# A residual block with two mixers: sums of squares over partitions taken from two rounded parts

## The reference

```python
mod = silu(c) @ w_ada + b_ada; shift, scale, gate = split(mod, 3)
h = rms_norm(x, g_pre) * (1 + scale) + shift
hq, hf, hi, hg, dq, dk, dv, dg, ma, mb = split(h @ w_in)
# branch A, 4 heads: gated linear recurrence, 128 x 128 state
o_a = rms_norm(hgrn2_chunked(hq, k(hf), hi, log_f(hf)), hg_norm_gain) * silu(hg)
# branch B, 4 heads: softmax(q1 k1) v - lam * softmax(q2 k2) v, causal
o_b = rms_norm(diff_attention(dq, dk, dv, lam), diff_norm_gain) * (1 - lam_init) * silu(dg)
y = (sigmoid(ma) * (o_a @ w_branch_a) + sigmoid(mb) * (o_b @ w_branch_b)) @ w_out
return x + gate * rms_norm(y, g_post)
```

## Time and profile before

| | us |
|---|---|
| median of 3 runs | 891.16 (889.34 to 892.09) |
| the profiled execution, its own time | 888.69 |
| its span | 886.8 |
| TensorE busy | 843.5 (95%) |
| VectorE busy | 608.5 (69%) |
| GpSimd busy | 478.4 (54%) |
| ScalarE busy | 471.7 (53%) |

### The profile page before, as it was taken

The page is one execution under the profiler, slowest core; times in us unless marked ns, Lnnn a source line. Parts: engine busy times, 40 slices in busy tenths (PEclk is TensorE's granted clock), DMA queues, the critical chain, the costliest instruction groups (busy, mean ns, idle before and its releaser), DMA issues. The chain is left out here.

```text
span 886.8 us, 13086 instructions
## 1 busy us (share of the span) xinstructions
PE 843.5 (95%) x4781; PEld 664.3 (75%) x4781; DVE 608.5 (69%) x712; ACT 471.7 (53%) x861; POOL 478.4 (54%) x363
## 2 busy tenths in 40 slices
PE   2899889999999999999999999999999999999997
PEld 2687678777777777777777777777788888887885
DVE  3888984788794888694897866864500166697775
ACT  7676323786443875445865336745455641333453
POOL 6054685455464455554545653566787822236884
PEclk9899899999999999999999999999999999999999
DMA  9914131102101101110120121021211561302222
GB/s 327 342 45 147 50 94 48 49 1 72 49 15 58 48 14 59 49 48 24 48 72 1 49 72 32 17 72 49 71 48 48 180 224 47 95 24 95 96 95 95
DMA packets 75586, 68.11 MB, mean 77 GB/s; under 512 B 3652, under 2 KB 65156, under 8 KB 75524
## 3 DMA queue, kind: packets, MB, share of 16 engines
q1 hardware_dynamic: 75408, 67.25, 23.6%
q10 hardware_dynamic: 116, 0.03, 0.0%
HBM read 58.88 MB, written 8.39 MB: 76 GB/s over the span
## 5 line engine op out<-in xcount | busy, mean ns | idle before, releaser
L624 POOL TENSOR_TENSOR w_lo<-w_raw,w_hi 128x512 fp32r<-128x512 f32 x140 | 193.5, 1384 | 258.7 <-ACT w_hi L1197 257.2
L935 PE MATMUL pj<-b_hi,w_hi 128*128 128x512 f32 x712 | 299.7, 421 | 6.3 <-DVE dk L1599 3.4
L937 PE MATMUL pj<-b_hi,w_lo 128*128 128x512 f32 x712 | 279.6, 393 | 0.0
L936 PE MATMUL pj<-b_lo,w_hi 128*128 128x512 f32 x712 | 279.0, 392 | 0.0
L935 PEld LDWEIGHTS pj<-b_hi,w_hi 128*128 128x128 f32 x712 | 134.4, 189 | 49.3 <-issue 12.5
L937 PEld LDWEIGHTS pj<-b_hi,w_lo 128*128 128x128 f32 x712 | 134.2, 188 | 30.0
L936 PEld LDWEIGHTS pj<-b_lo,w_hi 128*128 128x128 f32 x712 | 134.8, 189 | 25.6 <-issue 3.1
L1197 ACT ACTIVATE w_hi<-w_raw 128x512 fp32r<-128x512 f32 x132 | 82.8, 627 | 63.5 <-PE pj L937 57.4
L605 POOL TENSOR_TENSOR w_raw<-w_raw,w_raw 128x512 f32<-128x512 f32 x66 | 91.2, 1382 | 2.9
L685 POOL TENSOR_TENSOR wb_lo<-wb_raw,wb_hi 128x512 fp32r<-128x512 f32 x16 | 22.7, 1422 | 63.3 <-ACT wb_hi L1267 63.3
L1212 ACT ACTIVATE p<-sp,cols 128x1024 f32<-128x1024 f32 (+7 forms) x64 | 46.9, 738 | 0.8
(11 more groups left out here) (290 smaller groups left out, 1647.3 us busy)
## 6 DMA issues: line engine op xcount, KB each, us to landing
w_raw<-in_w_in SPq DMA_DIRECT2D x96, 256.0 KB, 4.1
x_in<-in_x SPq DMA_DIRECT2D x8, 512.0 KB, 7.2
ada<-in_w_ada SPq DMA_DIRECT2D x16, 256.0 KB, 7.1
ada<-in_w_ada SPq DMA_DIRECT2D x8, 512.0 KB, 8.0
ada_g<-in_w_ada SPq DMA_DIRECT2D x8, 512.0 KB, 3.9
res<-in_x SPq DMA_DIRECT2D x8, 512.0 KB, 4.4
out_x<-rows_o SPq DMA_DIRECT2D x7, 512.0 KB, 2.9
o_kepta<-oa SPq DMA_DIRECT2D x4, 512.0 KB, 6.0
```

What stands on the lines that cost most here:

```text
L624: pool.tensor_tensor(w_lo[slot(v)][:, :], raw[:, :], w_hi[slot(v)][:, :].bitcast(F32), ALU.subtract).then_inc(s_wlo, 1)
L935: pe.matmul(bank[:, :], wh, part(bh, kk), start=(fresh and kk == 0), stop=False, skip_group_check=True)
L936: pe.matmul(bank[:, :], wh, part(bl, kk), start=False, stop=False, skip_group_check=True)
L937: last = pe.matmul(bank[:, :], wl, part(bh, kk), start=False, stop=(kk == 3), skip_group_check=True)
```

## The change

The sums over partitions (two `ssa` and two `ssb` for each of four heads, 16 in all) were one float32 matmul of 128x512 with `ones`. Now ACT rounds the squares to fp32r (`sqa_hi`, `sqb_hi`), DVE subtracts that from the squares (`sqa_lo`, `sqb_lo`, written over the squares), and PE adds both parts with two fp32r matmuls with `ones_r`. `ones_r` is a rounded copy of `ones`, made once by ACT near the start. The sums move: `ssa` from 61, 63 to 62, 64 and `ssb` from 34, 50 to 35, 52; the first `over` of the recurrence from 63 to 65, the second half of the attention's norm from `over` 51, root 53, `finish` 54 to 53, 55, 56. The buffers of the new parts lie in space that other steps use, and waits are added for that.

```diff
-SSB_AT = (34, 50)
-CLIPB_AT, SQB_AT, OVERB_AT, ROOTB_AT, FINB_AT = (30, 45), (31, 46), (42, 51), (45, 53), (46, 54)
+SSB_AT = (35, 52)
+SQH_A_AT, SQL_A_AT, SQL_B_AT = (60, 61), (61, 62), (33, 49)
+CLIPB_AT, SQB_AT, OVERB_AT, ROOTB_AT, FINB_AT = (30, 45), (31, 46), (42, 53), (45, 55), (46, 56)
-VT_AT, KT_AT, ST_AT, O_AT, SSA_AT = (21, 26), (50, 51), (53, 54), (56, 57), (61, 63)
-CLIPA_AT, SQA_AT, OVERA_AT, ROOTA_AT, FINA_AT = (58, 59), (59, 60), (63, 70), (73, 73), (75, 76)
+VT_AT, KT_AT, ST_AT, O_AT, SSA_AT = (21, 26), (50, 51), (53, 54), (56, 57), (62, 64)
+CLIPA_AT, SQA_AT, OVERA_AT, ROOTA_AT, FINA_AT = (58, 59), (59, 60), (65, 70), (73, 73), (75, 76)
...
                 elif name == "ssa":
-                    pe.wait_ge(s_sqa, 2 * h + n + 1)
-                    last = pe.matmul(by[:, :], ones[:, :], k[:, n * HALF:(n + 1) * HALF], start=True, stop=True)
+                    pe.wait_ge(s_sqal, 2 * h + n + 1)
+                    pe.matmul(by[:, :], ones_r[:, :], part(sqa_hi, n), start=True, stop=False)
+                    last = pe.matmul(by[:, :], ones_r[:, :], part(sqa_lo, n), start=False, stop=True)
                 elif name == "ssb":
-                    pe.wait_ge(s_sqb, 2 * h + n + 1)
-                    last = pe.matmul(bx[:, :], ones[:, :], (sig, p1)[n][:, 0:HALF], start=True, stop=True)
+                    pe.wait_ge(s_sqbl, 2 * h + n + 1)
+                    pe.matmul(bx[:, :], ones_r[:, :], sqb_hi[h][n][:, :], start=True, stop=False)
+                    last = pe.matmul(bx[:, :], ones_r[:, :], sqb_lo[n][:, :], start=False, stop=True)
...
+            act.wait_ge(s_const, N_CONST)
+            act.activation(ones_r[:, :], ones[:, :], ACT.Copy).then_inc(s_sigc, 1)
...
+                    if h:
+                        act.wait_ge(s_unit["ssa"], 2 * h)
                     act.activation(part(v_tok, n), bx[:, :], ACT.Copy).then_inc(s_xa, 1)
...
+                for h, e in recurrence(m, SQH_A_AT):
+                    act.wait_ge(s_unit["o"], 2 * h + 2)
+                    act.wait_ge(s_sqa, 2 * h + e + 1)
+                    act.activation(part(sqa_hi, e), part(k, e), ACT.Copy).then_inc(s_sqah, 1)
...
                     act.activation(t, t, ACT.Square, scale=DOWN).then_inc(s_sqb, 1)
+                    if e == 0 and h < HEADS - 1:
+                        act.wait_ge(s_oah, 2 * h + 2)
+                    if h == HEADS - 1:
+                        act.wait_ge(s_unit["pv" if e else "o"], (NT if e else 2) * HEADS)
+                    elif e:
+                        act.wait_ge(s_unit["ssb"], 2 * h + 1)
+                    act.wait_ge(s_sqb, 2 * h + e + 1)
+                    act.activation(sqb_hi[h][e][:, :], t, ACT.Copy).then_inc(s_sqbh, 1)
...
+                        if h:
+                            dve.wait_ge(s_unit["ssb"], 2 * h)
...
+                for h, e in recurrence(m, SQL_A_AT):
+                    dve.wait_ge(s_sqah, 2 * h + e + 1)
+                    dve.tensor_tensor(part(sqa_lo, e), part(k, e), part(sqa_hi, e).bitcast(F32), ALU.subtract).then_inc(s_sqal, 1)
+                for h, e in attention(m, SQL_B_AT):
+                    dve.wait_ge(s_sqbh, 2 * h + e + 1)
+                    dve.tensor_tensor(sqb_lo[e][:, :], (sig, p1)[e][:, 0:HALF], sqb_hi[h][e][:, :].bitcast(F32),
+                                      ALU.subtract).then_inc(s_sqbl, 1)
```

More of the change, by code:

```diff
@@ L240, in build @@
         v_tok = block_at("v_tok", 40)
+        sqa_hi = block_at("sqa_hi", 40, 1, F32R)
+        sqa_lo = block_at("sqa_lo", 37, 1, F32R)
         f2 = block_at("f2", 41, 0.5)
@@ L255, in build @@
         sig = block_at("sig", 54, 0.5)
+        sqb_hi = [[block_at("sqb_hi", 41.5, 0.5, F32R)] * 2] * (HEADS - 1)
+        sqb_hi.append([block_at(f"sqb_hi_last{e}", (39, 50)[e], 0.5, F32R) for e in range(2)])
+        sqb_lo = [block_at("sqb_lo0", 54, 0.5, F32R), block_at("sqb_lo1", 49, 0.5, F32R)]
         vec_rows = block_at("vec_rows", 52, 1, F32, [P, P])
@@ L295, in build @@
         ones = small("ones", P)
+        ones_r = small("ones_r", P, F32R)
         cols = small("cols", 256)
@@ L383, in build @@
         s_sqa = sem("s_sqa")
+        s_sqah, s_sqal = sem("s_sqah"), sem("s_sqal")
+        s_sqbh, s_sqbl = sem("s_sqbh"), sem("s_sqbl")
         s_rva, s_rvb = sem("s_rva"), sem("s_rvb")
@@ L452, in y_free @@
                 eng.wait_ge(s_unit["dvt"], 2 * HEADS)
-            elif e == 5:
+            elif e == 6:
+                eng.wait_ge(s_unit["ssb"], 2 * HEADS - 1)
+            elif e in (2, 5):
                 eng.wait_ge(s_unit["ssa"], 2 * HEADS)
@@ L1549, in _ @@
             dve.wait_ge(s_gain, 1)
-            dve.wait_ge(s_sigc, 3)
+            dve.wait_ge(s_sigc, 4)
             dve.wait_ge(s_const, N_CONST)
```

## The result

The changed kernel takes **918.27 us** (median of 4 runs, 916.48 to 920.48), the kernel before in the same runs 891.62 us (4 runs, 889.34 to 892.23): the ratio is 1.0317, with a 95% interval of 1.0291 to 1.0342 (the two medians alone give 1.0299). The execution that was profiled took 920.48 us, with a span of 918.6 us.

A forecast was written before the change was run, and what follows sets the result against it. It took TensorE's instruction stream as the bound, busy 843.5 of 886.8 us. The terms -3.8 + 15.8 + 9.0 + 12.4 + 0.2 = +33.6 us gave 922.3 or 924.8, said as 923 us; range 907 to 934.

The forecast's parts named there:

- The matmuls, -3.8: PE's 16 sums: 0.40 us saved each, 6.4 in all, less 2.6 given back by three in slot 50; net -3.8 us.
- The first sum of the recurrence, +15.8: Slot 62, four heads: PE waits 3.95 us each for parts whose rounding stands behind the exponentials on ACT; +15.8 us.
- Slots 52 to 57, +9.0: Heads two to four: PE waits 1.8 us for states at first outputs, 1.2 for `oa` at second; +9.0 us.
- The clock, +12.4: Behind slot 62's four waits: each brings a fall of the granted clock to 0.50, costing 3.1 us; +12.4 us.
- `ones_r`, +0.2: Near the start: one 128x128 copy on ACT, 0.1 to 0.3 us, taken as +0.2.
- DVE's subtraction for slot 35, "0 to 0.3, three times, taken as 0": DVE's subtraction in slot 33 ends just about when PE comes to slot 35; 0 to 0.3 us, taken as 0.
- the sum by it, 3.5 us lower: The sum if the Trainium skill's under 1% held: clock penalty at most 8.9 us in all, the sum 3.5 us lower.
- the signs listed: Idle time of some 3.7 us at slot 62, waits in slots 56 and 57, new matmuls 0.23 us apart, low clock.
- The low clock for some 6 us behind each: Sign: granted clock 0.50 for some 6 us behind each of the four waits in slot 62.
- "Four more digits below 9": Sign: four more digits below 9 in the profile's row of PE's clock over 40 slices.
- The rival without falls of the clock: Waits come in slots 62, 56 and 57, clock stays: +21.2 us, 910 to 912; chance 0.12 with fewer or no falls.

The follow-up runs named there:

- filled kernel: The changed kernel with 14 more matmuls on PE ahead of the recurrence's first sum in each head, output the same: 910.13 us, ratio 1.0234 to the kernel before.
- second execution: The changed kernel run once more, with nothing altered: 917.92 us, ratio 1.0317 to the kernel before.
- better version: Against the kernel before, only `ssa` in slot 64 and `ssb` in slot 35 split, 8 of 16 sums: 886.54 us (ratio 0.9961), again 886.04 (0.9976).

## Why the prediction was right, and where not

The forecast was 923.0 with a range of 907 to 934, slower; 918.3 came. Mechanism, places and sign were right; one term was too large.

- **The matmuls, -3.8:** the ledger gives -3.7 (13 x -0.88, 13 x 0.45, 3 x 0.62). A float32 sum at 0.86 and two rounded at 0.46 are borne out by the kernel with doubled sums. That the three of slot 50 give nothing is in the ledger.
- **The first sum of the recurrence, +15.8:** 15.5 in four waits of 4.04, 3.82, 3.84 and 3.81. That it is the rounding's place behind the exponentials is shown by the kernel that puts it ahead of them.
- **Slots 52 to 57, +9.0:** 4.8 + 3.7 = 8.5 by the ledger, with waits of 1.6 (taken: 1.8) and 1.2 (taken: 1.2). The kernel with the moves alone shows them without any rounding.
- **The clock, +12.4:** the term that was mis-sized. Behind the four new waits four falls came, as taken; the waits of 1.6 and 1.2 brought none. But the four cost 8.5 us and not 12.4. The term took each at the 6.6 us of the earlier trace rows, all of it behind the wait. Two lasted 3.4 us, and of the 6.8 us of the long ones 1.4 and 1.1 us lay in the idle time, where a slow clock costs nothing. Half of what lies behind the wait, 5.5 and 5.7 us and twice 3.3 to 3.4, is 2.7 to 2.9 and 1.7; the filled kernel shows 2.6, 2.7 and 1.6. So the price was right (3.1 of 6.6 us is 0.47, and so are the measured ones), and the length behind the wait was mis-sized. For the short ones the prediction had no row, though the trace of before has one, at 50 to 53 us (granted clock 0.50).
- **`ones_r`, +0.2:** nothing in the ledger stands against it; it is too small to be seen in a start that varies by 1 us.
- Not in the sum: some 0.2 us in each slot 62, which the filled kernel has too. Its slots 62 and 63 cost 3.61; add the 0.87 saved in slot 63, take off 0.45 for the pair and 3.82 for the wait.
- **DVE's subtraction for slot 35, "0 to 0.3, three times, taken as 0":** it came as 0.17, which makes the pair 0.62 in place of 0.45 (counted with the matmuls above). In heads 1 to 3 DVE ends `sqb_lo` 0.15 us ahead of the pair, and the pair starts 0.32 us behind the matmul ahead of it, not 0.23. In the last head `sqb_lo` is done 2.5 us ahead, and the pair takes 0.45. The list of waits shows no idle time as short as this. From the timeline of the changed kernel, first head:

```profile
238.77 0.69 DVE L1780 TENSOR_TENSOR sqb_lo<-sig,sqb_hi 128x512 fp32r<-128x512 f32 x1
239.29 0.39 PE L950 MATMUL pj<-b_hi,w_lo 128*128 128x512 f32 x1
239.61 0.47 PE L831 MATMUL bx<-sqb_hi,ones_r 128*128 128x512 f32 x1
```

So -3.7 + 15.5 + 8.5 + 8.5 + 0.8 = 29.6 us come of the change, with 29.2 at the end of the second execution's ledger and 26.7 and 28.5 as the differences of the medians. Against 33.6, it is the clock's 3.9 that was too much. The Trainium skill ("TensorE: Matmul & The Clock Gate", section "What's actually happening") puts the penalty of the ramp under 1% of a typical kernel's span. The prediction set that against its own price, and the sum by it, 3.5 us lower, would have been nearer. The four falls that the change adds cost 8.5 of 918.6 us, 0.93%, so by themselves they agree with it. With the others the kernel may well be over it: half of the 3.4 us at the low clock behind each of the waits that end at 98 and 116 us, an estimate at the measured price, makes 11.9 us and 1.3%. The mean granted clock of the whole span is 0.979 (before 0.988), so at most 2.1% is lost in all, with what lies in idle time.

Of the signs listed, the waits in the timeline came as told. The low clock for some 6 us behind each came twice, and 3.4 us the other two times. "Four more digits below 9" in the clock's row did not come: two did, for the falls of 6.8 us. One of 3.4 us takes 7% off a slice of 23 us, and the digit stays 9. The rival without falls of the clock (910 to 912) is what the filled kernel measured, 910.1: the time that it gave was right, the condition did not hold.

## What to carry to other kernels

Before an operand is split, rounded or otherwise prepared for a cheaper matmul, look where each preparing step stands in its engine's order: here an instruction of 0.6 us behind 2.2 us of exponentials cost some 22 us in four places, where the whole change had at best 6.6 us to gain. Look as well at what a moved step now stands in front of: moving one sum and the norm's steps behind it by two slots, with nothing rounded, cost 11.0 us by the ledger. Take the saving only at the places where the parts are ready before TensorE is, and check the next wait down the chain, because it takes back what is saved ahead of it (slots 50 and 61 here). When a wait does come, price two things: the wait, and half of the time at the low clock that lies behind it.

## What the runs showed that was not expected

**Falls of different lengths.** Waits of the same length (3.81 to 4.08 us) brought falls of 3.4 us and of 6.8 us. In the first execution of the changed kernel the long ones came in heads 1 and 3, in the second in heads 2 and 4, and with the reciprocal moved all four were short. What decides it was not found; a fall here is better priced as between 1.6 and 2.7 us. Nor does every fall stand behind a wait: the one of before at 50 to 53 us came after 1.95 us of matmuls of one column, with no idle time of even 0.3 us ahead of it in the 8 us before.

**The first head's stretch.** With no instruction moved there, the way from slot 28 to slot 59 took 2.2 us more in one execution of the changed kernel, 0.0 in the other, and up to 4.8 more in other kernels (the 2.6 us in the ledger are those 2.2 and a later start). The wait for `dq`, in the timeline of PE before:

```profile
115.17 0.50 PE L935 MATMUL pj<-b_hi,w_hi 128*128 128x512 f32 x1 [0.78 <-DVE dq L1599]
```

In the changed kernel, first execution, POOL and DVE, and then PE:

```profile
107.99 1.69 POOL L635 TENSOR_TENSOR w_lo<-w_raw,w_hi 128x512 fp32r<-128x512 f32 x1 [1.51 <-ACT w_hi L1212]
...
108.47 2.30 DVE L1800 SCALAR_TENSOR_TENSOR acc_g<-ada_g,cols,acc_g 128x1024 f32<-128x1024 f32 x1
```

```profile
116.38 0.80 PE L948 MATMUL pj<-b_hi,w_hi 128*128 128x512 f32 x1 [2.96 <-DVE dq L1628]
```

DVE's `acc_g` step took 2.30 us where the same step takes 1.27 in the execution of before (at 108.49), and `dq` came 1.2 us later; behind the wait of 2.96 us the clock was at 0.50 in its turn (116.3 to 119.7 us). In the changed kernel POOL's `w_lo` has been running since 107.99 when the step starts; before, POOL is idle then, and its `w_lo` starts at 108.97. The 13 profiled executions divide in just this way. In seven a POOL instruction was running when the step started: the step took 2.29 to 2.31 us, PE waited 2.96 to 2.97 us for `dq`, and the way to slot 59 took 1.9 to 4.8 us more. In six POOL was idle at its start: the step took 1.27 or 1.28, the wait was 0.7 to 1.0, and the way to slot 59 was the same to 0.15 us. That POOL's instruction lengthens DVE's is argued from this and not tested, and why it starts earlier in some executions was not found.

These 1.9 to 4.8 us are as much as the better version gains or more, and the 24 runs of before in the last group lie between 886.58 and 894.84: only the better version's own 24 runs in two groups let it be told from nothing. Both of its profiled executions have the step of 2.3 us and the one of before has not, so its ledger is read from slot 60 on.
